# Cutting the first input blocks finer and moving the token positions behind the tiles of x

## The reference

```python
h = rmsnorm(x, g_mix[l])
u = h @ w_in[l]                       # 1024 channels -> 1440 columns
y_mla = mla_attention(u[..., :o1], u[..., o1:o2], u[..., o2:o3], positions, ...)
y_conv = conformer_conv(u[..., o3:], ...)
x = x + jnp.concatenate([y_mla, y_conv], axis=-1) @ w_out[l]
x = x + memory_cross_attention(rmsnorm(x, g_xattn[l]), rmsnorm(mem, g_mem[l]), ...)
x = x + moe_ffn(rmsnorm(x, g_ffn[l]), ...)          # 32 experts, top 4
```

## Time and profile before

| | us |
|---|---|
| median of three runs | 1153.33 |
| the profiled execution, its own time | 1153.83 |
| its span | 1152.1 |
| PE busy in the span | 1130.9 (98%) |
| PE idle in the first 20 us (page's windows: 17.39 busy) | 2.6 |
| granted TensorE clock, mean | 0.997 of full speed |
| memory read | 436.18 MB, 379 GB/s over the span |

### The profile page before, as it was taken

How to read it: one execution, slowest core, us unless ns; L and a number is a source line. 1 busy time by engine, 2 the same in 40 slices (tenths; PEclk the granted TensorE clock), 3 DMA queues, 4 the chain that set the end, 5 groups by cost and what they waited for, 6 DMA issues and landing times.

```text
span 1152.1 us, 16029 instructions
## 1 busy us (share of the span) xinstructions
PE 1130.9 (98%) x5376; PEld 502.2 (44%) x5377; DVE 358.9 (31%) x933; ACT 221.7 (19%) x429; POOL 85.2 (7%) x206
## 2 busy tenths in 40 slices
PE   9999999999999999999999999999999999999999
PEld 6785487653333333333333333333333333333333
DVE  6898413232222222222222222222222222222223
ACT  5321213121111121111111111111111111111113
POOL 2990000000000000000000000000000000000000
PEclk9999999999999999999999999999999999999999
DMA  9464336389999999999999999999999999999995
GB/s 364 188 272 176 146 146 282 156 347 429 429 435 431 427 433 433 427 432 433 396 421 437 437 422 433 437 432 423 437 437 424 431 437 433 424 426 429 424 426 244
DMA packets 28821, 437.76 MB, mean 380 GB/s; under 512 B 4017, under 2 KB 4657, under 8 KB 12017
## 3 DMA queue, kind: packets, MB, share of 16 engines
q1 hardware_dynamic: 27920, 436.10, 89.4%
q10 hardware_dynamic: 864, 1.14, 0.3%
HBM read 436.18 MB, written 1.05 MB: 379 GB/s over the span
## 4 chain that ended last, share of the span: by engine, by line
PE 77%; DMA 20%; SPq 1%; ACT 1%; issue 0%; DVE 0%; ACTq 0%; DVEq 0%
PE bank L1813 28%; DMA ring<-in_w_up_dram 20%; PE bank L1858 16%; PE total L1773 4%; PE bank L1760 4%; PE bank L1452 2%; PE bank L1471 2%; PE bank L1866 2%; PE bank L1683 2%; PE bank L1462 2%; PE bank L1767 1%; PE bank L1617 1%; PE total L1617 1%; DMA ring<-in_w_in_dram 1%; PE bank L1911 1%; PE bank L1576 1%
## 5 line engine op out<-in xcount | busy, mean ns | idle before, releaser
L1813 PE MATMUL bank<-ring,buf_m 128*64 128x512 f32 (+1 forms) x2192 | 465.2, 581 | 13.4 <-DMA ring<-in_w_up_dram 13.3
L1813 PEld LDWEIGHTS bank<-ring,buf_m 128*64 128x64 f32 x2192 | 156.9, 138 | 316.1 <-issue 286.4
L1858 PE MATMUL bank<-ring,buf_m 128*64 128x512 f32 x1056 | 239.9, 595 | 0.0
L1343 DVE COPY buf_f<-bank 128x512 f32<-128x512 f32 x32 | 22.1, 692 | 448.6 <-PE bank L1813 448.6
L1858 PEld LDWEIGHTS bank<-ring,buf_m 128*64 128x64 f32 x1056 | 72.8, 136 | 136.5 <-issue 126.5
L888 ACT ACTIVATE buf_m<-buf_f 128x256 f32<-128x256 f32 x32 | 13.3, 416 | 333.1 <-DVE buf_f L1353 333.1
L1773 PE MATMUL total<-buf_m,wr_sb 64*128 64x512 f32 x272 | 67.6, 615 | 1.6 <-ACT buf_m L897 0.8
L656 POOL TENSOR_TENSOR buf_v<-table,buf_v 128x4 f32<-128x4 f32 x33 | 6.6, 201 | 775.6 <-DVE buf_v L1331 775.3
L1760 PE MATMUL bank<-buf_k,buf_v 128*64 128x512 f32 x264 | 63.9, 605 | 0.0
L1349 DVE TENSOR_TENSOR buf_f<-bank,buf_v 128x512 f32<-128x512 f32 x64 | 44.0, 687 | 57.7 <-PE bank L1866 57.7
L897 ACT ACTIVATE buf_m<-bank,buf_v 128x512 f32<-128x512 f32 x32 | 22.0, 687 | 194.1 <-PE bank L1858 194.1
(11 more groups left out here) (389 smaller groups left out, 884.4 us busy)
## 6 DMA issues: line engine op xcount, KB each, us to landing
ring<-in_w_up_dram SPq DMA_DIRECT2D x48, 4096.0 KB, 30.0
ring<-in_w_down_dram SPq DMA_DIRECT2D x24, 4096.0 KB, 30.4
ring<-in_w_up_dram SPq DMA_DIRECT2D x29, 2048.0 KB, 15.3
ring<-in_w_down_dram SPq DMA_DIRECT2D x13, 2048.0 KB, 38.2
ring<-in_w_down_dram SPq DMA_DIRECT2D x6, 1024.0 KB, 10.8
ring<-in_w_up_dram SPq DMA_DIRECT2D x6, 1024.0 KB, 38.5
ring<-in_w_in_dram SPq DMA_DIRECT2D x4, 1024.0 KB, 17.2
ring<-in_w_xkv_dram SPq DMA_DIRECT2D x2, 2048.0 KB, 27.4
```

The costliest lines, as they stand in the source:

```text
L1813: ins = t_.matmul(banks[bank][h * 64:(h + 1) * 64, c0:c1], xg[:, k, :], w[:, :, k % 4, h, :], start=first, stop=last)
L1858: ins = t_.matmul(banks[2][h * 64:(h + 1) * 64, :], actT[:, f, :], group(slot_of(at))[:, lo + h * BANK:lo + (h + 1) * BANK], start=f == 0, ...
```

## The change

`FIRST` has six pieces instead of five: blocks 0, 1, 2 and 3 alone, then 4-5 and 6-7. SP issues four pieces of weights (the same four blocks as before) ahead of x0 and x1, and the positions behind x0 and x1 instead of ahead of them. DVE gains four pieces instead of three ahead of its wait for the positions; these are again blocks 0 to 3.

```diff
-FIRST = [(0, 1), (1, 2), (2, 4), (4, 6), (6, 8)]
+FIRST = [(0, 1), (1, 2), (2, 3), (3, 4), (4, 6), (6, 8)]
...
             load_pair(0)
             load_pair(1)
             load_pair(2)
-            sp.dma_start(pos_i, positions[0].rearrange("(a p) -> p a", p=P), allow_slow_non_contiguous=True).then_inc(loaded["pos"], 16)
+            load_pair(3)
             for t in range(TT):
                 sp.dma_start(xs[:, t, :], x[0, t * P:(t + 1) * P, :]).then_inc(loaded[f"x{t}"], 16)
-            load_pair(3)
+            sp.dma_start(pos_i, positions[0].rearrange("(a p) -> p a", p=P), allow_slow_non_contiguous=True).then_inc(loaded["pos"], 16)
             load_pair(4)
+            load_pair(5)
...
             dve.wait_ge(loaded["by_channel"], 16)
-            for i in range(3):
+            for i in range(4):
                 gained(i)
             dve.wait_ge(loaded["pos"], 16)
             dve.wait_ge(const_ready, 21)
...
             angle(0, 0.25)
             dve.wait_ge(const_ready, N_CONST)
-            gained(3)
             gained(4)
+            gained(5)
             rstd("x", 0, D)
```

More of the change, by code:

```diff
@@ L269, in wait_drained @@
             eng.wait_ge(drained[drained_at[job][0]], drained_at[job][1])
-        names = ["x0", "x1", "mem", "memT", "pos", "by_channel", "xT0", "xT1", "xT2", "xT3", "xT4", "wu0", "wu1", "wu2", "wu3", "wu4",
+        names = ["x0", "x1", "mem", "memT", "pos", "by_channel", "xT0", "xT1", "xT2", "xT3", "xT4", "xT5", "wu0", "wu1", "wu2", "wu3", "wu4", "wu5",
                  "wc0", "wc1", "wc2", "wc3", "uq", "ukv", "wk0", "wk1", "wv", "wout", "wxq0", "wxq1", "wxo", "bdown", "router", "bup", "late"]
```

## The result

The changed kernel takes 1158.88 us, the median of six runs (1156.26 to 1159.97), against 1153.62 us (1152.59 to 1154.60) for the kernel before: ratio 1.0041, interval 1.0030 to 1.0052. It is slower by 5.3 us. The profiled execution took 1159.97 us with a span of 1158.3, 6.2 us longer than the span before, and is the longest of the six; in a second set of six runs (among the experiments) the median was 1158.07 us. The changed kernel spreads over 4 us from run to run, the kernel before over 2.

What follows compares the result with a forecast made beforehand. PE, busy 1130.9 us, bounds the kernel, with the last part paced by a DMA stream that PE sets going. Delay 2.2 plus clock 1.7 gives +3.9 us on the profiled run; median forecast 1157.2 us, range 1154.6 to 1159.6.

Steps and rivals of the forecast that it cites:

- Where a delay at the start goes: Trunk to experts: a shift of the whole trunk moves the DMA stream and the end by the same amount.
- The finer pieces are worth nothing alone and cost nothing alone: Blocks 2 and 3 at the start: second pair at 8.9 instead of 9.91 us, but the gap only moves before block 4.
- The positions land at 12.3 and DVE stands before the CAST: SP's queue and DVE: positions land last, at 12.3 us (10.7 to 13.7); the CAST starts about 12.35, 2.6 us later.
- the same bytes in smaller packets: Loads at the start: cost of splitting them into smaller packets, bounded by 0 and 0.5 us, taken as 0.1.
- The third pair 2.2 us later: PE at blocks 4-5: starts at 15.55 instead of 13.36 us, because DVE gains these blocks 2.6 us later.
- The clock, 1.7 us: PE after 3.9 us of idleness before blocks 4-5: the granted clock falls to the lower level, costing 1.7 us.
- case C: Rival at the start: two slow clock stretches or later positions, 5.6 or 5.3 us, about 1158.8 us; chance 18 in 100.
- The sum: Whole kernel: 2.2 us of delay plus 1.7 us of clock, +3.9 us, median 1157.2 us; chance 50 in 100.
- Case B: Rival at DVE's wait: positions land in time, by 9.8 us, so not slower, 1153.3 or 1152.9 us; chance 7 in 100.
- case D: Rival in the experts: their waits for the DMA swallow the delay, about 1153.8 us; chance 5 in 100.
- Case A: Rival at the start: the delay of 2.2 us comes but PE's clock stays up, 1155.5 us; chance 20 in 100.

Runs made afterwards that it cites:

- the pure delay: Kernel before plus 14 extra 128x128 products on PE ahead of the first convolution products, keeping PE at work 3.05 us longer: 1157.06 us, ratio 1.0030.

## Why the prediction was right, step by step

- *Where a delay at the start goes:* in full to the end. Right: 6.2 us at the convolution products and 6.2 us in the span; +3.4 for +3.4 in the pure delay. In other executions the expert stage added up to 1.0 us of its own.
- *The finer pieces are worth nothing alone and cost nothing alone:* right, 0.9999. The second pair started at 9.28, not 8.9, since DVE could start block 2 only at 8.80 instead of 8.1; block 3 it started at 10.60 instead of 9.2. With the positions in their old place DVE started them at 7.65 and 9.04, a little before the forecast.
- *The positions land at 12.3 and DVE stands before the CAST:* the mechanism is right, and with the five old pieces so is the number, 12.35. In the changed kernel it is 13.23 (13.2 to 14.3 in the four profiles of it and of its copy with extra products). The term that was mis-sized is "the same bytes in smaller packets", taken as 0.1 us and bounded by 0.5: it is 0.9 us on the positions. The forecast of 12.3 was a sum of three transfers that was to be kept, with the tiles 1.5 us earlier. In the changed kernel the last of the weights ahead of the tiles landed 1.8 us later than the 6.8 taken, the tiles at 10.3 and 12.3 as before, and the positions 0.9 behind them. With five pieces the tiles came earlier, at 9.1 and 11.0, and the positions at 12.3, close to the sum as it was argued.
- *The third pair 2.2 us later:* 3.1 us, by that 0.9.
- *The clock, 1.7 us:* the slow stretch came where it was forecast, but the profiled executions show 2 x 3.4 us less the idle part, 5.92 - 3.03 = 2.9 us on the third pair and 0.2 on rx, the case called C. Over all runs the price lies lower, at 0.4 to 1.7. The argument from the length of the idleness was weaker than it looked: it left out the wait of 2.22 us that cost nothing. Nor does PE's idleness reach the 3.9 us forecast; it was 3.4 and 3.74 us.
- *The sum:* +3.9 forecast, +5.3 and +4.4 measured in the two sets. The time, 1158.88, lies in the range, but it is the number of case C, 1158.8, and not the 1157.2 of the forecast; the profiled execution lies 2.3 us above the 1157.7 given for it, with both terms larger at once, 3.1 and 3.1 us. So what was right is the mechanism, and both of its sizes were low in the profile. Case B (positions in time) is refuted by the kernel with the positions alone moved, +3.3 us, and case D (swallowed) by the pure delay, which arrives whole. Case A had 1155.5 us for a clock that stays up; the changed kernel with extra products, whose clock stays up at the start, took 1158.12 and 1157.68, with its positions later than A assumed.

## What to carry to other kernels

Before moving a small transfer to the back of a queue, read what stands behind its wait on the engine that takes it: here one KB decided about ten small instructions and, behind them, PE's next blocks, and moving one instruction out from behind that wait gave back two thirds of the loss with the transfer as late as before. A longer idleness of PE can cost a second time by the clock, but a profile that shows this may be the worst run of its kernel, so the price is to be taken from medians, and from more runs than the five to twelve per kernel here. Before arguing from one wait of a trace, look for waits of the same length with another outcome. Finer pieces gain nothing where the piece that PE waits for last keeps the same bytes ahead of it.

## What the runs showed of the hardware

- With six pieces and the tiles of x directly behind four 208 KB loads, the 16 DMA engines were at 0.86 of their time and 264 GB/s from 6 to 8 us in the changed kernel, and at 0.85 to 0.96 and 258 to 323 GB/s in four other profiles with the same loads; with 256 integers between them (357 GB/s), or the last two loads joined (378 GB/s), they were full.
- PE's granted clock at the start fell for one stretch of 3.4 us (third pair 4.75 us) after 1.95, 2.07 and 2.99 us of idleness, for twice as long (5.92 us) after 3.4 and 3.74 us, and after 1.81 us not at all. In the expert stage it stayed up after 2.22 us in one place and 3.52 us in another, and fell after 2.21 us: the length of the idleness alone does not decide.
- With the same order of loads the positions landed at 13.1 to 14.3 us in five profiles: 13.2 twice in the changed kernel, 13.1 with block 4-5 gained first, 13.9 and 14.3 with extra products on PE.
